# A value projection fed from a turned copy of x instead of from transposes on TensorE

## What is computed

```python
def rmsnorm(x, g):
    xf = x.astype(jnp.float32)
    y = xf * lax.rsqrt(jnp.mean(xf * xf, axis=-1, keepdims=True) + EPS)
    return (y * g.astype(jnp.float32)).astype(x.dtype)
...
        h = rmsnorm(x, mix_norm[layer])
        proj = h @ w_in[layer]
        hq, hf, hi, hg, rq, rk, rv, rg, ga, gb = jnp.split(proj, split_at, axis=-1)
```

## Time and profile before

| | before |
|---|---|
| median of three runs | 1434.91 us (1433.55 to 1435.89) |
| span of the profiled execution | 1432.1 us |
| PE busy in the span | 1385.4 us, 97% |
| DVE busy | 898.8 us, 63% |
| ACT busy | 645.8 us, 45% |
| last product of the changed stage starts | 151.28 us |

### The profile page before, as it was taken

How to read it: one execution, slowest core, us unless ns; L and a number is a source line. 1 busy time by engine, 2 the same in 40 slices (tenths; PEclk the granted TensorE clock), 3 DMA queues, 4 the chain that set the end, 5 groups by cost and what they waited for, 6 DMA issues and landing times. The chain is left out here.

```text
span 1432.1 us, 19078 instructions
## 1 busy us (share of the span) xinstructions
PE 1385.4 (97%) x7705; PEld 1156.2 (81%) x7705; DVE 898.8 (63%) x1190; ACT 645.8 (45%) x835; POOL 77.5 (5%) x71
## 2 busy tenths in 40 slices
PE   7999999999999999999999999996999999999997
PEld 5888778887888788888878889985788888877886
DVE  5510166658887576655563443348799999889574
ACT  4410222213333433333351121244688888888565
POOL 0000000000000000000000000002122222221000
PEclk9999999999999999999999999997999999999999
DMA  6200111015443621232353337314999999996231
GB/s 251 87 3 1 51 31 31 16 31 165 125 123 103 265 59 51 69 117 89 118 160 107 103 118 248 128 69 170 386 370 385 391 383 389 378 371 238 105 138 47
DMA packets 114089, 231.60 MB, mean 162 GB/s; under 512 B 13776, under 2 KB 73808, under 8 KB 99408
## 3 DMA queue, kind: packets, MB, share of 16 engines
q1 hardware_dynamic: 103456, 209.11, 41.4%
q0 software_dynamic: 9248, 16.80, 3.1%
q10 hardware_dynamic: 1296, 4.46, 0.8%
HBM read 200.97 MB, written 41.94 MB: 170 GB/s over the span
## 5 line engine op out<-in xcount | busy, mean ns | idle before, releaser
L1694 DVE TENSOR_TENSOR two_chunk_lo<-two_chunk_raw,two_hi 128x2048 fp32r<-128x2048 f32 x96 | 217.3, 2287 | 21.1 <-ACT two_hi L1690 21.1
L1690 ACT CAST two_hi<-two_chunk_raw 128x2048 fp32r<-128x2048 f32 x96 | 181.1, 1916 | 9.8 <-DMA two_chunk_raw<-w_e 9.2
L2917 PE MATMUL two_banks<-two_hi,two_xT_hi 128*128 128x512 f32 x256 | 103.2, 403 | 2.8 <-DVE two_xT_lo L2110 2.3
L2919 PE MATMUL two_banks<-two_hi,two_xT_lo 128*128 128x512 f32 x256 | 100.5, 393 | 0.0
L2918 PE MATMUL two_banks<-two_chunk_lo,two_xT_hi 128*128 128x512 f32 x256 | 100.4, 392 | 0.0
L1383 ACT CAST mix_w_hi<-mix_w_raw 128x512 fp32r<-128x512 f32 x72 | 44.7, 621 | 104.6 <-PE front_sums L1609 67.0
L466 PE MATMUL vals_sums<-vals_w_hi,mix_hT_hi 128*128 128x512 f32 x192 | 76.7, 399 | 2.2 <-DVE vals_w_lo L391 1.2
L1495 DVE TENSOR_TENSOR mix_w_lo<-mix_w_raw,mix_w_hi 128x512 fp32r<-128x512 f32 x72 | 49.6, 689 | 45.9 <-ACT mix_w_hi L1383 45.4
L2783 PE MATMUL two_banks<-mix_y_hi,mix_w_hi 128*128 128x512 f32 x192 | 74.8, 390 | 2.1 <-PEq L146 2.1
L1607 PE MATMUL front_sums<-two_T_hi,mix_w_hi 128*128 128x512 f32 x192 | 75.3, 392 | 1.2 <-issue 1.2
L468 PE MATMUL vals_sums<-vals_w_hi,mix_hT_lo 128*128 128x512 f32 x192 | 75.8, 395 | 0.0
(11 more groups left out here) (359 smaller groups left out, 3342.3 us busy)
## 6 DMA issues: line engine op xcount, KB each, us to landing
two_chunk_raw<-w_e SPq DMA_DIRECT2D x102, 1024.0 KB, 17.4
mix_w_raw<-w_in SPq DMA_DIRECT2D x44, 512.0 KB, 3.8
quarter_sums<-two_T_buf_lo SPq DMA_DIRECT2D x32, 256.0 KB, 2.5
sigs<-two_staged SPq DMA_DIRECT2D x8, 1024.0 KB, 5.0
two_sig<-sigs SPq DMA_DIRECT2D x16, 512.0 KB, 4.5
two_r<-results SPq DMA_DIRECT2D x16, 512.0 KB, 4.8
vals_w_raw<-w_in SPq DMA_DIRECT2D x12, 512.0 KB, 8.0
heads_values<-x SPq DMA_DIRECT2D x8, 512.0 KB, 10.6
```

What stands on the lines that cost most here:

```text
L1690: self.nc.scalar.copy(self.high(n)[:], self.raw(n)[:]).then_inc(self.hi_ok, 1)
L1694: self.nc.vector.tensor_tensor(self.low(n)[:], self.raw(n)[:], self.high(n)[:].bitcast(F32), ALU.subtract).then_inc(self.lo_ok, 1)
L2917: nc.tensor.matmul(sums, xT_hi[u][:, k, :], hi[:, cols], start=(k == 0), stop=False)
L2919: mm = nc.tensor.matmul(sums, xT_lo[u][:, k, :], hi[:, cols], start=False, stop=(k == last))
```

## The change

x is also given to the kernel transposed, as `x_t` (1024 channels by 1024 tokens). Eight further loads of 512 KB bring it in, one for each tile, in pieces of 128 floats (512 bytes), into the memory that `hT_lo` has later (`raw`). The norm weight comes as a 128x8 column table. PE does no transposes in this stage. On DVE each half tile of `raw` is first multiplied by the norm weight, which is one number for a partition and slice (`by_gain`), and later by the reciprocal root, which varies along the row (`by_rstd`). That vector is made equal on all partitions by PE: DVE multiplies the identity by the tile's reciprocal roots (`diagonal`), and a matmul of ones with it writes the row into PSUM (`spread_rstd`). The sum of squares still comes from the row tiles of x (`root_of`), which are still loaded.

Tiles 0, 1 and 2 of block 0 are multiplied before their roots are known: `plain_high` and `plain_low` split the weighted but unscaled tile into spare buffers, and `store` multiplies by the reciprocal root when it copies the result out. Their scaled `hT` is made at the end of block 0, after tiles 3 to 7. PE begins with ten matmuls of ones (`warm_up`). The lists of SP, ACT, DVE and PE are written anew:

```diff
--- before.py
+++ after.py
@@ -230,36 +230,65 @@
 
     W, BLOCKS, QUARTERS = 512, (HI, RV, RV + 512), 4
     KQ = KT // QUARTERS
+    ROWS = (0, 3, 1, 4, 2, 5, 6, 7)
+    UNSCALED = 3
+    SCALED = (3, 4, 5, 6, 7, 0, 1, 2)
...
         ring_raw, ring_hi, ring_lo = kept["weight_slots"]
+        raw = nc.alloc_sbuf_tensor_at("vals_xT_raw", [P, KT, S], F32, offset=kept["hT_lo_at"])
         w_hi = m.sb("w_hi", [P, 2, KT, W], F32R)
...
-        gain_row = m.sb("gain_row", [P, D])
+        gain = m.sb("gain", [P, KT])
+        ones, diag = m.sb("ones", [P, P]), m.sb("diag", [P, 2, P])
...
-        turned = kept["sums"][:].rearrange("p u a b -> p u (a b)").rearrange("p u (k c) -> p u k c", c=P)
+        spread = kept["sums"][:].rearrange("p u a b -> p (u a) b")
         sums = m.ps("sums", [P, 4, W])
...
+
+        plain_hi = [ring_hi[:, 0], ring_hi[:, 1], flat(w_hi[:, 1, 0:2, :])]
+        plain_lo = [ring_lo[:, 0], ring_lo[:, 1], flat(w_hi[:, 1, 2:4, :])]
...
+            def load_xT(t):
+                src = dram["x_t"].rearrange("(k p) s -> p k s", p=P)[:, :, t * P:(t + 1) * P]
+                sp.dma_start(raw[:, :, t * P:(t + 1) * P], src).then_inc(xT_in[t], 16)
 
...
+            load_xT(0)
+            sp.dma_start(gain[:], dram["mix_norm_col"]).then_inc(gain_in, 16)
+            load_w(0, 0)
+            load_w(0, 1)
+            load_w(0, 2)
+            load_xT(1)
+            load_w(0, 3)
+            load_xT(2)
+            sp.dma_start(ident[:], dram["ident"]).then_inc(ident_in, 16)
             load_x(0)
-            sp.dma_start(gain_row[:], dram["mix_norm_row"].to_broadcast([P, D])).then_inc(gain_in, 16)
-            sp.dma_start(ident[:], dram["ident"]).then_inc(ident_in, 16)
-            load_w(0, 0)
+            load_x(3)
+            load_xT(3)
             load_x(1)
-            for n in range(1, QUARTERS):
-                load_w(0, n)
-            for t in range(2, TT):
+            load_x(4)
+            load_xT(4)
+            load_x(2)
+            for t in range(5, TT):
                 load_x(t)
+                load_xT(t)
...
-            def square(t):
+            def plain_high(t, half):
+                act.wait_ge(gained, gained_at(t, half))
+                nc.scalar.copy(plain_hi[t][:, half_of(half), :], of_tile(raw, t, half)).then_inc(plain_hi_ok, 1)
+
+            def root_of(t):
                 act.wait_ge(x_in[t], 16)
-                if t:
-                    act.wait_ge(summed, t)
+                if row_of(t) > 1:
+                    act.wait_ge(summed, row_of(t) - 1)
                 nc.scalar.activation(ring_raw[:, 0].rearrange("p k c -> p (k c)"), x(t), ACT.Square,
                                      accum_out=stat[:, 0, t:t + 1]).then_inc(summed, 1)
-
...
-            def high(t, halves=(0, 1)):
-                for half in halves:
-                    act.wait_ge(turned_ok, 2 * t + half + 1)
-                    ks = slice(4 * half, 4 * half + 4)
-                    nc.scalar.copy(hT_hi[:, ks, t * P:(t + 1) * P], turned[:, t % 2, ks, :]).then_inc(hT_hi_ok, 1)
+            def high(t):
+                for half in range(2):
+                    act.wait_ge(scaled, scaled_at(t, half))
+                    nc.scalar.copy(of_tile(hT_hi, t, half), of_tile(raw, t, half)).then_inc(hT_hi_ok, 1)
 
             def store(b, t):
                 act.wait_ge(full, group(b, t) + 1)
                 col = b * W
-                nc.scalar.copy(values[:, t, col:col + W], sums[:, group(b, t) % 4, :]).then_inc(stored[0], 1)
+                out, src = values[:, t, col:col + W], sums[:, group(b, t) % 4, :]
+                if b == 0 and t < UNSCALED:
+                    act.wait_ge(rstd_ok, row_of(t))
+                    nc.scalar.activation(out, src, ACT.Copy, scale=stat[:, 3, t:t + 1]).then_inc(stored[0], 1)
+                    return
+                nc.scalar.copy(out, src).then_inc(stored[0], 1)
...
-            root(0)
-            high(0, (0,))
+            plain_high(0, 0)
             first_step()
             second_step()
-            high(0, (1,))
-            for n in range(1, QUARTERS):
-                weights(0, n)
...
-                    high(t + 1)
-                if t + 2 < TT:
-                    square(t + 2)
-                    root(t + 2)
-                if t >= 4:
-                    weights(1, t - 4)
-                if t % 2 == 0:
-                    store(0, t)
-            act.wait_ge(summed, TT)
+            plain_high(0, 1)
+            weights(0, 1)
+            weights(0, 2)
+            plain_high(1, 0)
+            plain_high(1, 1)
+            weights(0, 3)
+            plain_high(2, 0)
+            plain_high(2, 1)
+            root_of(0)
+            root_of(3)
+            store(0, 0)
+            high(3)
+            root_of(1)
+            root_of(4)
+            high(4)
+            root_of(2)
+            store(0, 2)
+            root_of(5)
+            high(5)
+            weights(1, 0)
+            root_of(6)
+            high(6)
+            store(0, 4)
+            root_of(7)
+            weights(1, 1)
+            high(7)
+            high(0)
+            weights(1, 2)
+            high(1)
+            store(0, 6)
+            weights(1, 3)
+            high(2)
...
-            def scale(t):
-                dve.wait_ge(summed, t + 1)
-                nc.vector.tensor_scalar(stat[:, 1, t:t + 1], stat[:, 0, t:t + 1], 1.0 / D, EPS,
-                                        ALU.mult, ALU.add).then_inc(mean_ok, 1)
-                dve.wait_ge(rooted, t + 1)
-                nc.vector.reciprocal(stat[:, 3, t:t + 1], stat[:, 2, t:t + 1]).then_inc(rstd_ok, 1)
-                dve.wait_ge(rstd_ok, t + 1)
...
+            def by_gain(t):
+                dve.wait_ge(xT_in[t], 16)
                 if t == 0:
                     dve.wait_ge(gain_in, 16)
                 for half in range(2):
-                    cols = slice(half * HALF, (half + 1) * HALF)
-                    nc.vector.scalar_tensor_tensor(out=x(t)[:, cols], in0=x(t)[:, cols], scalar=stat[:, 3, t:t + 1],
-                                                   in1=gain_row[:, cols], op0=ALU.mult, op1=ALU.mult).then_inc(scaled, 1)
-
...
-            def low(t, halves=(0, 1)):
-                for half in halves:
-                    dve.wait_ge(hT_hi_ok, 2 * t + half + 1)
-                    ks = slice(4 * half, 4 * half + 4)
-                    nc.vector.tensor_tensor(hT_lo[:, ks, t * P:(t + 1) * P], turned[:, t % 2, ks, :],
-                                            hT_hi[:, ks, t * P:(t + 1) * P].bitcast(F32), ALU.subtract).then_inc(hT_lo_ok, 1)
+                    part = of_tile(raw, t, half)
+                    V.tensor_tensor(part, part, bc(gain[:, half_of(half)], 2, P), ALU.mult).then_inc(gained, 1)
+
+            def plain_low(t, half):
+                dve.wait_ge(plain_hi_ok, 2 * t + half + 1)
+                V.tensor_tensor(plain_lo[t][:, half_of(half), :], of_tile(raw, t, half),
+                                plain_hi[t][:, half_of(half), :].bitcast(F32), ALU.subtract).then_inc(plain_lo_ok, 1)
+
+            def rstd(t):
+                dve.wait_ge(summed, row_of(t))
+                V.tensor_scalar(stat[:, 1, t:t + 1], stat[:, 0, t:t + 1], 1.0 / D, EPS,
+                                ALU.mult, ALU.add).then_inc(mean_ok, 1)
+                dve.wait_ge(rooted, row_of(t))
+                V.reciprocal(stat[:, 3, t:t + 1], stat[:, 2, t:t + 1]).then_inc(rstd_ok, 1)
+
+            def diagonal(t):
+                j = SCALED.index(t)
+                dve.wait_ge(rstd_ok, row_of(t))
+                if j == 0:
+                    dve.wait_ge(ident_in, 16)
+                if j >= 2:
+                    dve.wait_ge(spread_ok, j - 1)
+                V.tensor_scalar(diag[:, j % 2, :], ident[:], stat[:, 3, t:t + 1], None, ALU.mult).then_inc(diag_ok, 1)
+
+            def by_rstd(t):
+                j = SCALED.index(t)
+                dve.wait_ge(spread_ok, j + 1)
+                dve.wait_ge(gained, gained_at(t, 1))
+                if t < UNSCALED:
+                    dve.wait_ge(plain_lo_ok, 2 * t + 2)
+                for half in range(2):
+                    part = of_tile(raw, t, half)
+                    V.tensor_tensor(part, part, bc(spread[:, j % 4, 0:P], 1, 4), ALU.mult).then_inc(scaled, 1)
+
+            def low(t):
+                for half in range(2):
+                    dve.wait_ge(hT_hi_ok, scaled_at(t, half))
+                    V.tensor_tensor(of_tile(hT_lo, t, half), of_tile(raw, t, half), of_tile(hT_hi, t, half).bitcast(F32),
+                                    ALU.subtract).then_inc(hT_lo_ok, 1)
...
-
-            nc.vector.memset(warm[:], 1.0).then_inc(warmed, 1)
-            scale(0)
-            low(0, (0,))
+                out, src = values[:, t, col:col + W], sums[:, group(b, t) % 4, :]
...
+            by_gain(0)
+            plain_low(0, 0)
             first_step()
             second_step()
-            low(0, (1,))
```

(100 more changed lines are left out.)

79 lines of the change are left out of this document (42 added, 37 removed).

## The result

| | before | after |
|---|---|---|
| median of seven runs | 1434.91 us (1431.77 to 1435.89) | 1438.29 us (1437.31 to 1443.1) |
| span of the profiled execution | 1432.1 us | 1435.5 us |
| PE busy | 1385.4 us | 1384.9 us |
| DVE, ACT busy | 898.8, 645.8 us | 912.4, 650.3 us |
| SP let go at block 0's end | 64.66 us | 67.76 us |

A forecast was written before the change was run, and what follows sets the result against it. PE was taken as block 0's bound, DVE's list after the change: 26.2 + 38.1 = 64.3, so block 1 at 66.0 instead of 64.66, +1.4 us, 1434.9 to 1436.3 us; 8-in-10 range 1430.5 to 1439.6.

The forecast's parts named there:

- rival 2: In tiles 0 and 1 PE's clock rises late: at 20 us 1438.1 us in all, at 22 us 1439.1; 19%.
- rival 4: Turned x loads much slower than in the earlier trace: 2.5 us each gives 1437.4, 3 us or more 1438.4; 3%.
- The start: Start of block 0: first turned load in at 4.7 to 4.9, first product at 7.65 instead of 10.60.
- The loads: First loads: 1.54 to 1.6 us a turned tile, 1.30 a weight quarter; end moves -0.3 to +1.1 us.
- Tile 0: Block 0's first tile: last quarter ready at 16.35, PE waits 2.0 us, tile ends at 17.8.
- From the first `by_rstd` to the last diagonal: DVE's list in block 0 runs without slack: operations and waits together 38.1 us, from 26.2 to 64.3.
- the waits for ACT's sums: In DVE's list in block 0: waits for tiles 1, 4, 2, 5, 6 and 7, 6.1 us in all.
- rival 3: DVE's operations don't overlap when waiting on its own counts or reading PSUM: 0.69 each, 1438.5 us; 7%.
- PE's waits: In block 0 PE waits 9 us, before tiles 4, 5, 6 and at the diagonals of tiles 5, 0, 1, 2.
- Rival 1: In block 0 PE stays the bound: block 1 starts at 57.1, 1427.4 us in all; 12%.
- milder version: DVE's list with fewer waits in block 0: saving half of them gives 1432.6 us; a part within the 15% for faster.

The follow-up runs named there:

- The first experiment: Changed kernel with the norm-weight multiply on DVE cut to a 128x4 operation for tiles 3 to 7: block 1 at 64.54, 1436.76 us, ratio to before 1.0012.
- the third: Changed kernel with the spread matmuls placed earlier in PE's program: block 1 at 63.70, 1437.07 us, ratio to before 1.0001.
- the seventh: Changed kernel with weight quarters loaded ahead of tile 1, roots one tile earlier and spreads moved: block 1 at 59.12, 1430.75 us, ratio to before 0.9968.
- fourth: Changed kernel without its ten warming matmuls: block 1 at 68.19, 1441.9 us, ratio to before 1.0038.
- twelfth experiment: Changed kernel with quarters first, roots and spreads earlier, and sixteen warming matmuls instead of ten: block 1 at 59.04, 1431.17 us, ratio to before 0.9972.
- sixth: Changed kernel with squares and roots asked for one tile earlier in ACT's and DVE's lists: block 1 at 66.70, 1438.54 us, ratio to before 1.0017.
- the second experiment: Changed kernel with the turned x stored tile by tile in DRAM: block 1 at 67.70, 1440.2 us, ratio to before 1.0037.

## Why the forecast held in kind and fell short in size

**The mechanism: right.** PE's saved transposes are there, DVE becomes the bound of block 0, and waits between the three lists eat more than what was saved. The first experiment (DVE's work cut, 3.2 us earlier with PE's work unchanged), the third and the seventh show it from three sides. The number is partly luck: the range reached up to 1439.6 only because it took in rival 2, a late clock, and in after's profile the clock was not late. What made the time longer than forecast was the loads, for which the sum had allowed at most +1.1 us and rival 4 had 3%.

**The start: 7.65, measured 8.04.** The first half of tile 0 was multiplied at 5.22, not at 4.9, since the gain table landed at 5.1 (DVE's idle before 5.22 ends with it).

**The loads: the term that was too small.** The sum let tile 0 land at 4.9 and then one load after the other at the plateau's rates, 404 GB/s for weights and 340 for 512-byte pieces. It had the third quarter, `load_w(0, 2)`, in at 8.8 and tile 1 at 10.3. They landed at 10.18 and 11.89. Two things make up tile 1's 1.6 us, about in equal parts.

The first is the rate. The rows from 4.8 to 10 us, before and then after:

```profile
DMA packets 889, 1.82 MB, mean 350 GB/s; under 512 B 73, under 2 KB 201, under 8 KB 889
```

```profile
DMA packets 1542, 1.83 MB, mean 352 GB/s; under 512 B 52, under 2 KB 848, under 8 KB 1542
```

The row of the kernel before was there to be read ahead of the prediction. After's first 10 us in 40 slices, then their sum:

```profile
GB/s 0 0 0 0 0 0 0 76 41 188 260 293 340 344 348 236 129 218 337 385 393 393 344 287 303 311 360 320 352 369 401 381 356 350 342 317 336 358 354 350
DMA packets 2817, 2.54 MB, mean 254 GB/s; under 512 B 212, under 2 KB 2032, under 8 KB 2817
```

The mean of 254 counts the first 1.75 us, in which nothing had arrived yet; in every kernel here these are 1.5 us or more. The bytes of the first load were through at 3.96 and those of all up to tile 1 at 10.23: 6.3 us, where the sum has 5.4 between the two landings.

The second is the landing itself. The trace has sixteen semaphore counts for each load, one from each DMA engine, and the load is in with the last. Tile 1's first count came at 9.99, its eighth at 10.85, its last at 11.89. So it landed 1.65 us after its bytes and those ahead of it had moved as a total, when 3.21 MB had come and it needed 2.63. For the first load, from which the sum starts, that lag was 0.97 us. In the kernel before it was 1.1 for the first load and 0.7 to 0.9 for the next ones; for the load in tile 1's place it was 0.9 to 2.0 in the variants, and 2.5 in the one with long pieces alone, where the sixteen counts lay 3 us apart. Why one engine's share comes so late, and why the rate stays at 325 to 365 GB/s from 4.8 to 10 us in all kernels, stays open: stride, piece length and the small table's place don't remove either.

Through DVE's list tile 1's lateness went on whole: `by_gain(1)` at 11.91 instead of 10.38 (16.35 less the 5.97 of work behind it), the last quarter ready at 17.89 instead of 16.35, tile 1 at 19.43 instead of 17.8, the first spread at 27.60 instead of 25.9, block 1 at 67.76 instead of 66.0. The fourth rival looked in the right place but for another thing: it took the turned loads to be slower than the earlier trace rows over the whole stage and found 2.5 us a tile harmless. Their rate was as in the earlier trace rows (347 GB/s from 10 to 15 us). What counted was the landing of one load of eight, the one for which DVE stands while a weight quarter waits behind.

**Tile 0: one gap of 2.0 us predicted, three of 1.46, 1.70 and 1.82 measured.** The clock was at its upper level from 8.04 on, so PE ran through each quarter in less time and waited for the next. The end of the tile depends on the last quarter alone, as the forecast said.

**From the first `by_rstd` to the last diagonal: 38.1 predicted, 37.8 measured** (28.02 to 65.80). Its terms hold singly too: DVE's starts of 128x512 are 0.60 apart (each pair of multiplies lasts 1.28 to 1.29 from start to end, one alone 0.68 to 0.69, with the gain's broadcast column and with PSUM's row alike); the diagonal costs 0.20 (33.13 to 33.34); the waits for ACT's sums in this stretch are 5.6, six of the seven that make up the 6.4 of the table above (the prediction says 6.1; its six terms add up to 6.2); DVE's idle before the first spread is 5.45 (5); the spread costs PE 0.15 (27.36 to 27.74, less a product's 0.23), for which the sum had 0.16. This settles rival 3: operations overlap also where an operand is in PSUM. (The 2.2 us at which the prediction priced it fit the 22 multiplies of the stretch; 0.09 us on all 37 operations would be 3.3.)

**PE's waits: 9 us predicted, 9 measured from start to start, 5.9 in the waits' rows** (3.4 and 2.5). The profile counts idle time from the modelled end of a matmul, some 0.2 us after the next could have started, so a few tenths are missing for each wait. PE's program from the first spread to block 1 took 40.2 us (27.60 to 67.76), the sum 40.1 (25.9 to 66.0). In it stand 132 products at 0.227 and eight spreads at 0.15, 31.1 us of work.

**Rival 1, PE the bound: no.** Its milder version, DVE's list with fewer waits, is near what the same work gives in another order (59.12), by an earlier start of the chain as much as by shorter waits.

**Rival 2, the clock: an execution's luck, and mostly hidden.** In after's profile it rose before the first product; in most of the variants' it was low at the first product and rose between 11 and 17 us. In tile 0 that costs nothing that can be seen (fourth and twelfth experiment). In tile 1 it costs 0.2 us a product, 1.35 in all before the first spread (sixth), by the mechanism that the rival names. The Trainium skill ("TensorE: Matmul & The Clock Gate", What's actually happening) says that the number of matmuls at the lower clock varies from run to run of one kernel. No kernel was profiled twice, so no run here shows quite that; nearest are after and the second experiment, whose programs for PE are the same: the clock rose before 8.0 us in one and at 13.4 in the other.

**The remaining 0.3 us and the scatter of whole runs.** After's three runs of 1441 us and more are those with a mean granted clock of 0.986 or less; the four others, 1437.3 to 1438.3 us, have 0.988 to 0.991. One place where the clock falls is to be seen in a later stage, where the gate's heads are turned. First before, then after (timeline, and the window of 10 us from there):

```profile
470.76 1.09 PE L1590 MATMUL gate_turned<-kept_ident,heads_values 128*128 128x128 f32 x8 [2.21 <-DVE heads_values L1459]
```

```profile
470.00:480.00 10.00, 9.23 (x44) 7.65 (x45) 6.73 (x8) 4.86 (x7) 0.00 (x0) 1.00 0.90 298
```

```profile
474.03 1.97 PE L1731 MATMUL gate_turned<-kept_ident,heads_values 128*128 128x128 f32 x8 [2.21 <-DVE heads_values L1600]
```

```profile
473.00:483.00 10.00, 8.97 (x37) 7.67 (x38) 6.99 (x8) 5.12 (x7) 0.00 (x0) 0.83 0.87 287
```

The same 2.21 us of idle come ahead of the same eight transposes. In one kernel the clock stays at 1.00, in the other it falls to a mean of 0.83, and 1.3 us are lost by the 36th product behind the transposes. The code there is unchanged. At the end of the spans the two kernels are only 3.4 us apart, so after makes up for most of it elsewhere. The profiles of the seventh and the twelfth variant begin block 1 within 0.1 us of each other and end at 1424.0 and 1431.8.

Such falls are commoner in the changed kernels, by the mean granted clock that each run has on record. It was 0.986 or less in 7 of 106 runs of the kernel before, in 3 of 7 of after and in 40 of 92 of the ten variants of after that have ten warming matmuls or none. But it was so too in 5 of 10 runs of the kernel before with ten warming matmuls, and in none of 12 with sixteen in the last variant. So the new lists aren't needed for it, and what brings it about isn't known. It means that whole times 0.1 or 0.2% apart say little of block 0, where the profile reads 3.10 us.

## What to carry to other kernels

When work moves from a full engine to one with 40% of idle time, don't add up busy times: walk the lists in order, since DVE was busy only 75% of the stretch in which it was the bound, and reordered lists turned the same instructions from 3.4 us of loss into a gain of 4 to 5. Lists that wait for each other must be moved together: asking for the roots earlier lengthened DVE's wait for spreads from 5.4 to 7.8 us until PE's program moved too. For loads in the first microseconds take the rate of the first microseconds of the kernel before, not that of its plateau. Don't take a load to be in when its bytes' turn has passed: read from the trace when its last share lands, and look for the one load for which an in-order engine stands.

## What the runs showed of the hardware

- In all fourteen profiles the queue moved next to nothing in the first 1.5 us and 325 to 365 GB/s from 4.8 to 10 us, with pieces of 512 bytes or 4 KB. From 10 to 15 us it moved 330 to 347 in the ten kernels that load turned tiles in 512-byte pieces then, 404 to 411 in the four that don't.
- A load of 512 KB is in when the last of sixteen DMA engines has counted. From the first count to the last it took 1.90 us for tile 1 in after, 0.5 for the loads from 7 us on in before, and 3 us in the kernel with long pieces.
- Beside a load of 4 KB in 128 pieces of 32 bytes the rate was 129 to 236 GB/s between 3.75 and 4.5 us in after, some 0.3 us of loading lost. With the table loaded first the dip came before 3 us.
- A float32 matmul of 128 columns is recorded as two instructions (twenty for the ten warming calls), 0.23 us apart at the lower clock.
- Behind a wait of 2.2 us of PE the clock was at 0.83 in the mean of 10 us in one execution and at 1.00 in another. With ten warming matmuls that end at 5.2 to 5.7 us the clock was up at the first product, at 8.0 and 8.4, in two profiles and low in the others; in one of the two it was low again from 9.7 us.
- DVE's 128x512 operations last 0.68 to 0.69 us each and start 0.60 apart, also for a broadcast operand and for an operand in PSUM.
